# The odd mixer of a two-layer transformer block: keys and values in front of the last query slot, whose product and head chain stand beside the attention's first steps

## The reference, cut to what matters

```python
def odd_mixer(h_lat, h_ctx, w_in, w_out, qg, kg, cos, sin, need_ctx_out):
    q, k, v = split_cols(h_lat @ w_in, SIZES_ODD)          # 1024, 256, 256 columns
    q = apply_rope(rms_norm(q.reshape(B, S, H_C, HD_C), qg), cos, sin) * HD_C ** -0.5
    k = apply_rope(rms_norm(k.reshape(B, S, KV_C, HD_C), kg), cos, sin)
    v = v.reshape(B, S, KV_C, HD_C)
    ...
    ck, cv = split_cols(h_ctx @ w_in[:, H_C * HD_C:], SIZES_ODD[1:])
    ck = rms_norm(ck.reshape(B, L, KV_C, HD_C), kg)
    k_all = jnp.concatenate([ck, k], axis=1)
    v_all = jnp.concatenate([cv, v], axis=1)
    out_lat = block_attention(q, k_all, v_all) @ w_out     # softmax over 512 keys
```

## Time and profile before

| what | us |
|---|---|
| median of 3 runs (lowest, highest) | 1694.84 (1694.27, 1703.23) |
| the profiled execution's own time | 1694.8 |
| its span | 1693.2 |
| PE busy in it | 1547.2 (91%) |
| DVE busy | 577.5 (34%) |
| ACT busy | 341.5 (20%) |
| mean granted TensorE clock | 0.954 of full speed |

### The profile page before, as it was taken

One profiled execution on the slowest core, in us unless ns is written; L12 is line 12 of the kernel. 1 busy time (PEld: TensorE's weight loads), 2 busy tenths in 40 slices (PEclk: granted clock), 3 DMA queues, 4 the chain that ended last, 5 costly groups with the idle time before them and its releaser, 6 DMA issues.

```text
span 1693.2 us, 27222 instructions
## 1 busy us (share of the span) xinstructions
PE 1547.2 (91%) x11479; PEld 1107.5 (65%) x11479; DVE 577.5 (34%) x1412; ACT 341.5 (20%) x786; POOL 93.8 (6%) x144
## 2 busy tenths in 40 slices
PE   6999899999879999997896899999949898999997
PEld 5787678877734766655533799988836575655554
DVE  2614423333345238404515111111046643233333
ACT  1313211122141112115304000000142223010110
POOL 0010000000110000001100200000010000000000
PEclk9899999999989989997997999999979997999999
DMA  8365444556873431034520799999876032999996
GB/s 263 96 209 182 143 132 129 165 186 195 219 226 106 154 116 51 32 119 127 199 75 30 285 389 399 396 399 401 341 245 237 25 125 96 371 391 387 387 387 255
DMA packets 188232, 366.93 MB, mean 217 GB/s; under 512 B 19100, under 2 KB 145912, under 8 KB 172272
## 3 DMA queue, kind: packets, MB, share of 16 engines
q1 hardware_dynamic: 171552, 322.90, 53.6%
q0 software_dynamic: 10544, 32.48, 6.0%
q10 hardware_dynamic: 6048, 10.31, 1.7%
HBM read 345.26 MB, written 20.41 MB: 216 GB/s over the span
## 4 chain that ended last, share of the span: by engine, by line
PE 81%; DVE 8%; DMA 5%; ACT 3%; issue 2%; POOL 1%; SPq 0%; POOLq 0%; ACTq 0%; DVEq 0%
PE ps_proj L646 30%; PE ps_outp L646 10%; PE ps_proj L1210 8%; PE ps_outp L1210 8%; PE ps_score L1210 7%; PE ps_outp L1155 3%; DMA ring<-in_exp_w 3%; PE ps_turn L799 2%; PE ps_outp L1310 2%; PE ps_proj L772 2%; PE ps_score L817 1%; DVE both_probs L2142 1%; PE ps_score L646 1%; DMA ring<-in_w_in 1%; PE ps_score L869 1%
## 5 line engine op out<-in xcount | busy, mean ns | idle before, releaser
L646 PE MATMUL ps_proj<-h_t,ring 128*128 128x256 f32 (+1 forms) x1280 | 356.6, 438 | 8.0 <-DMA ring<-in_w_in 3.7
L646 PEld LDWEIGHTS ps_proj<-h_t,ring 128*128 128x128 f32 x1280 | 246.9, 195 | 112.0 <-issue 77.1
L1210 PE MATMUL ps_proj<-ring,arena 128*32 128x384 f32 (+2 forms) x1760 | 118.8, 386 | 6.3 <-ACT arena L1919 2.2
L1210 PEld LDWEIGHTS ps_proj<-ring,arena 128*32 128x32 f32 (+1 forms) x1760 | 103.9, 115 | 21.7 <-issue 12.6
L1210 PE MATMUL ps_score<-ring,arena 128*32 128x384 f32 (+2 forms) x1760 | 115.3, 381 | 1.3 <-DMA ring<-in_exp_w 1.3
L1210 PE MATMUL ps_outp<-ring,arena 128*32 128x384 f32 (+2 forms) x1504 | 112.7, 417 | 3.0 <-DVE arena L2523 2.1
L1210 PEld LDWEIGHTS ps_score<-ring,arena 128*32 128x32 f32 (+1 forms) x1760 | 98.4, 113 | 17.4 <-issue 8.9
L646 PE MATMUL ps_proj<-ring,h_t 128*128 128x256 f32 (+1 forms) x512 | 105.8, 364 | 0.4 <-ACT arena L1787 0.4
L1607 ACT ACTIVATE arena<-ps_proj 128x512 f32<-128x512 f32 (+1 forms) x68 | 39.0, 576 | 319.8 <-PE ps_proj L646 318.1
L646 PEld LDWEIGHTS ps_proj<-ring,h_t 128*128 128x128 f32 x512 | 92.1, 190 | 14.9 <-issue 3.5
L1210 PEld LDWEIGHTS ps_outp<-ring,arena 128*32 128x32 f32 (+1 forms) x1504 | 81.8, 114 | 26.5 <-DVE arena L2523 3.8
(11 more groups left out here) (354 smaller groups left out, 1844.9 us busy)
## 6 DMA issues: line engine op xcount, KB each, us to landing
ring<-in_exp_w SPq DMA_DIRECT2D x138, 1024.0 KB, 11.1
ring<-in_ada_w SPq DMA_DIRECT2D x48, 1024.0 KB, 5.6
ring<-in_w_in SPq DMA_DIRECT2D x30, 1024.0 KB, 6.3
arena<-in_exp_w SPq DMA_DIRECT2D x24, 1024.0 KB, 17.1
ring<-in_even_w_in SPq DMA_DIRECT2D x12, 1024.0 KB, 6.2
ring<-in_w_out SPq DMA_DIRECT2D x8, 1024.0 KB, 5.2
row_store<-in_exp_w SPq DMA_DIRECT2D x8, 1024.0 KB, 16.8
x_t<-in_exp_w SPq DMA_DIRECT2D x16, 512.0 KB, 16.4
```

Source lines behind the costliest of these rows:

```text
L646: last = pe.matmul(out, w, a, start=(i == 0), stop=(i == len(pairs) - 1))
L1210: last = pe.matmul(b[p0:p0 + pn, c0:c0 + wn], x_of(p0, lo, pn), w(w0, wn), start=first and p0 not in strip[:i], stop=done and p0 not in st ...
```

## The change

The six slots run in the order 0, 1, 2, 4, 5, 3 (`ODD_SLOTS`), and their weights are loaded in that order. The first five stand where they stood; the values and the fifth slot's `turn_pairs` follow; the sixth slot, the last pair of query heads (heads 6 and 7), moves into the attention. TensorE computes its product at the end of step 0 and its head sums and rotation at the end of step 2. ScalarE does its square and scaled copy behind the first softmax and its root behind the third. VectorE does its chain in step 3, between the copy of the transposes and the copy of the apply. The scores of head 0 wait for `head_ready` 13, those of head 6 for 14. The wait for the values' drain moves into the apply. `gv_slot` now marks the moved slot. No arithmetic is added or removed.

```diff
-        for c in range(6):
+        for c in (0, 1, 2, 4, 5, 3):
             add(((0, KC, 256), k_cols(dr["odd_w_in_2"][0], 256 * c, 256)))
...
+        ODD_SLOTS = (0, 1, 2, 4, 5, 3)
...
-            for c in range(6):
+            for s, c in enumerate(ODD_SLOTS[:5]):
...
-            mark["gv_slot"] = slot[0]
             token_major(h2, 4)
             k_gv = use["proj"]
-            turn_pairs(5)
-            got("proj", k_gv)
-            pe.wait_ge(head_ready, 14)
+            turn_pairs(4)
+
+            def last_queries():
+                mark["gv_slot"] = slot[0]
+                feature_major(h2, S, S)
+                mark["raw", 5] = use["proj"]
+
             units = []
             for h in range(8):
                 for t in range(NB):
                     def scores(h=h, t=t):
+                        if t == 0 and h in (0, 6):
+                            pe.wait_ge(head_ready, 13 if h == 0 else 14)
                         b = claim("score")
...
                     def apply(par, h=h):
+                        got("proj", k_gv)
                         b = claim("outp")
...
-            attention(units)
+            attention(units, {0: last_queries, 2: lambda: turn_pairs(5)})
...
+            def odd_slot(s):
+
+                b = take("proj")
+                if s >= 2:
+                    act.wait_ge(head_ready, 8 + s - 1)
+                head_square(b[:, :], g_sq)
+                row = ROW["gqa_q" if ODD_SLOTS[s] < 4 else "gqa_k"]
+                act.activation(raw[:, s % 2, :], b[:, :], ACT.Identity, scale=vec[:, row:row + 1]
+                               ).then_inc(drained["proj"], 1)
+
+            for s in range(5):
+                if s == 1:
                     rms_root(S)
                     stream_shift(1)
...
+                odd_slot(s)
+                if s >= 1:
+                    head_root(8 + s - 1, P, ODD_SLOTS[s - 1] >= 4)
             for t in (0, 2):
                 evac(gv[:, t:t + 2, :])
-            head_root(13, P)
+            head_root(12, P)
             warm_up(ACT.Exp)
-            for _ in range(16):
+            for i in range(16):
                 softmax([(0, T2)])
+                if i == 0:
+                    odd_slot(5)
+                if i == 2:
+                    head_root(13, P, False)
             warm_up(ACT.Sqrt)
...
-            for c in range(6):
-                dve.wait_ge(drained["proj"], mark["raw", c])
+            def turned_head(s):
+
+                c = ODD_SLOTS[s]
+                dve.wait_ge(drained["proj"], mark["raw", s])
                 b = take("outp")
...
+            for s in range(5):
+                turned_head(s)
...
-            attention(units)
+            attention(units, (range(3, 4), lambda part: turned_head(5)))
```

More of the change, by code:

```diff
@@ L1526, in _, with turn_pairs @@
             ready = mixer_input()
-            def turn_pairs(c):
+            def turn_pairs(s):
                 head_sums("ones", g_sq)
-                got("proj", mark["raw", c])
+                got("proj", mark["raw", s])
                 b = claim("outp")
-                chain(b[:, :], [(cst("rot2"), raw[:, c % 2, :])]).then_inc(filled["outp"], 1)
-            for c in range(6):
+                chain(b[:, :], [(cst("rot2"), raw[:, s % 2, :])]).then_inc(filled["outp"], 1)
+            for s, c in enumerate(ODD_SLOTS[:5]):
                 if c < 4:
@@ L1546, in _ @@
                         done_with("proj")
-                mark["raw", c] = use["proj"]
-                if c == 0:
+                mark["raw", s] = use["proj"]
+                if s == 0:
                     norm(h2[:, :, 0:S], S)(0, 4)
-                if c >= 1:
-                    turn_pairs(c - 1)
-            mark["gv_slot"] = slot[0]
+                else:
+                    turn_pairs(s - 1)
             token_major(h2, 4)
             k_gv = use["proj"]
-            turn_pairs(5)
-            got("proj", k_gv)
-            pe.wait_ge(head_ready, 14)
+            turn_pairs(4)
[3 more added lines that the diff above has]
+                mark["raw", 5] = use["proj"]
             units = []
@@ L2028, in _ @@
             stream_squares(1, mark["moe_done", 0])
-            for c in range(6):
-                if c == 1:
+            def odd_slot(s):
[8 more added lines that the diff above has]
+                if s == 1:
                     rms_root(S)
                     stream_shift(1)
[L2033 to L2041, removed]
+                odd_slot(s)
+                if s >= 1:
+                    head_root(8 + s - 1, P, ODD_SLOTS[s - 1] >= 4)
             for t in (0, 2):
                 evac(gv[:, t:t + 2, :])
-            head_root(13, P)
+            head_root(12, P)
             warm_up(ACT.Exp)
-            for _ in range(16):
+            for i in range(16):
                 softmax([(0, T2)])
+                if i == 0:
+                    odd_slot(5)
+                if i == 2:
+                    head_root(13, P, False)
             warm_up(ACT.Sqrt)
@@ L2786, in _ @@
             sin2 = cst("sin2").unsqueeze(1).to_broadcast([P, 2, S])
-            for c in range(6):
-                dve.wait_ge(drained["proj"], mark["raw", c])
+            def turned_head(s):
+                c = ODD_SLOTS[s]
+                dve.wait_ge(drained["proj"], mark["raw", s])
                 b = take("outp")
-                r = raw[:, c % 2, :]
-                rs = rsin[:, c % 2, :]
+                r = raw[:, s % 2, :]
+                rs = rsin[:, s % 2, :]
                 if c < 4:
@@ L2803, in _ @@
                     step(dve.tensor_tensor(r[:, lat], r[:, lat], rs[:, lat], ALU.add))
[L2804 removed]
+                head_rstd(8 + s)
                 dst = gq_t[:, 2 * c:2 * c + 2, :].rearrange("p a b -> p (a b)") if c < 4 else gk_t[:, c - 4, :]
                 dve.tensor_tensor(dst, r, rstd[:, :], ALU.mult).then_inc(head_ready, 1)
+            for s in range(5):
+                turned_head(s)
             units = []
```

## The result

The changed kernel took 1707.82 us (median of 20 runs, 1697.96 to 1714.16) against 1697.79 for the kernel before (20 runs, 1691.31 to 1706.91): ratio 1.0056, 95% interval 1.0043 to 1.0070. It is slower by 9.5 us, 7.3 to 11.9. The forecast was 1701.6, ratio 1.0040, and its range ended at 1707; the time lies above it. The profiled execution took 1701.29 us, with a span of 1699.7; of the 20 runs it is the second fastest.

What follows compares the result with a forecast made beforehand. TensorE carries 81% of the chain that ended last; the change acts only through its idle time. VectorE's stall +5.4 and the low clock +1.4 make +6.8 us on 1694.8: 1701.6 us, range 1694 to 1707.

Steps and rivals of the forecast that it cites:

- The hole: TensorE's idle time before the attention's first scores, filled by VectorE's key head chain: keeps 5.67 us, comes 8.62 us earlier.
- The moved product: Last query product, moved behind the attention's first scores: TensorE work costs the same on both sides, 6.90 us at full clock.
- The stall of step 3: Before transposes 3 TensorE idles 6.6 us (second idle time) for VectorE's 6.25 us head chain; +5.4 us up to there.
- The clock behind it: After TensorE's second idle time, before transposes 3: 3.45 us at 1.2 GHz make one step 3.9 us, +1.4 us.
- both clock terms: Low clock for 3.45 us after each restart: under the moved product until 1327.8, and behind the second idle time, +1.4 us.
- The rival of the low clock: Clock stays low through the attention's next steps, 1.4 us for each further step, giving 1704.4; chance 0.20.
- the base: Time of the kernel before: profiled execution 1694.8 us, taken as practically the median of the runs, 1694.84.
- within 0.5%: Whole kernel: chance 0.64 that the time changes by less than 0.5%, 8.5 us.
- -0.9 if the head chain cost nothing: Attention up to transposes 3: -0.9 us without VectorE's head chain cost, from the covered softmax of step 0.
- the ScalarE part: Moved slot's square, copy, root and table loads in the attention's first steps: covered, nothing; 3.3 us of cover at the root.
- Pass-through: From the attention's end to the kernel's end: a shift passes one to one, the stretch stays 315 us.

Runs made afterwards that it cites:

- early_turn: Kernel before with the last key head's sums, rotation and root moved in front of the values; 1691.34 us, ratio 0.9963.
- after_early: Changed kernel with the last key head's sums and rotation moved in front of the values; 1699.36 us, ratio 1.0006.
- chain_off: Changed kernel without the last query head pair's rotation and reciprocal on VectorE, four of five instructions; 1695.47 us, ratio 1.0002.
- double: Changed kernel with the last head's reciprocal done twice, 3.35 us more on VectorE in step 3; 1713.20 us, ratio 1.0071.
- late: Changed kernel with the last slot's head sums, rotation, root and VectorE chain at steps 8 and 9 instead of 2 and 3; 1705.99 us, ratio 1.0045.
- changed_again: The changed kernel measured once more without any edit; 1703.08 us, ratio 1.0048.
- order_only: Kernel before with the slots in the order 0, 1, 2, 4, 5, 3 and nothing moved into the attention; 1702.06 us, ratio 1.0015.

## Why the prediction was right or wrong

**The hole stays.** Right: 5.62 us for 5.67. It was VectorE's chain: early_turn, which only moves that chain's start, removes all but 0.69 us, the values' drain.

**The moved product costs the same on both sides.** Right at full clock: 6.90 forecast, 6.91 in after_early, and chain_off keeps the product and is level with before. In the changed kernel it takes 8.30, because it stands where the clock is low; the forecast had 7.76 there.

**The stall of step 3.** Right in place, cause and size. Forecast: transposes 3 at 1350.05 in the time of before; the stage started 0.69 us earlier after, so 1349.72 reads 1350.41 there, 0.36 late. Two small errors stand in that. TensorE was 0.68 late up to transposes 2, from the clock under the moved product, which came back 4.8 us behind the first scores and not 3.45. From transposes 2 to 3 it took 8.51 us and not the 8.83 that I had allowed. VectorE's five instructions took 6.25 us; double and late show that what stands in this chain is paid for in full, and in the middle of the attention too.

**The clock behind it. This is the step of the forecast that failed.** I carried the 3.45 us of low clock after the restart from the first idle time over to the second, for a term of 1.4 us, and put a longer one into a rival of 0.20. It was 6.0 us: the two steps took 4.32 and 3.27 for my 3.93 and 2.53, and the term is 2.54 us; 1.9 to 2.5 in the five profiles that have the stall without filling. The mistake was to count the low time from the restart. In before the clock had fallen 3.4 us before the first scores; in after it fell 0.9 us before transposes 3, so of the same 6.8 us of low clock more was left to be paid by the work. Nor is 6.8 us the same everywhere: it was 3.4 in the first low stretch of changed_again and 10.2 in order_only. So I could not have named the size from one row, only a wider bound. Why the clock falls late in one idle time and early in another no run here shows. With both clock terms the sum is 6.8 + 0.36 + 1.13 = 8.3, which is the 8.24 of the stretch. The rival of the low clock was thus half true: one further step, not two.

**The rest of the miss.** The time is 6.2 us over the forecast (1707.82 for 1701.6). Of that 3.0 is the base: I read 1694.84 as settled from three runs, of which one stood at 1703.23, and the median of 20 runs of the same kernel is 1697.79. 1.4 us are the two clock terms. The last 1.8 us, by which the two medians differ (10.0) more than the two stretches (8.24), no trace shows; the interval of 7.3 to 11.9 us holds the 8.24, and changed_again gives 1.0048 (8.1 us). The clock terms alone would have stayed inside the range; it needed all three to leave it, and it should have been wider on top by the scatter of the base. That the profiled execution took 1701.29 us, next to the forecast of 1701.6, is luck: it is 6.45 us over the profile of before, because it reached this stage 0.69 us earlier and took 1.05 us less behind it. The forecast of "within 0.5%" (0.64) was on the wrong side of the line by 0.06%; with the clock's term right it would have been 8.3 of 8.5 us, an even chance.

**"-0.9 if the head chain cost nothing".** Wrong. chain_off, with one fifth of the chain's instructions left, is 1.05 above before, not under it. Two things make up the difference of about 2 us. 1.3 is step 3: the reload of the exponential's table, which I had called covered, lies on the path as soon as VectorE's chain doesn't cover it. 0.7 is again the low clock under the moved product, longer than I had allowed. For the changed kernel itself the ScalarE part held: root at 1341.04, exponential at 1343.50, wanted at 1348.99. From its timeline of all engines:

```profile
1339.74 1.28 ACT L1614 ACT_TABLE_LOAD   x1 [1.05 <-PE ps_proj L647]
...
1341.04 0.60 ACT L1614 ACTIVATE root<-ps_proj 128x512 f32<-128x512 f32 x1
...
1343.50 0.69 ACT L1670 ACTIVATE both_probs<-ps_score,negmax 128x512 f32<-128x512 f32 x1
...
1348.99 0.15 DVE L2153 RECIPROCAL inv<-total 128x1 f32<-128x1 f32 x1
```

The rows show no drain beside the load here either (load at 1339.74, root 1.30 us later); the Trainium skill's 2.66 us for a switch (ScalarE: Activation LUTs, What ACT_TABLE_LOAD costs) is not borne out in these rows, and the measurement decides.

**Pass-through.** Right: 314.5 us from the attention's end to the span's end, 315 forecast, and 314 to 317 in nearly all kernels.

## What to carry to other kernels

Before moving work beside a loop, ask for every engine what room a step has, not only for the one that seems to bound the stage: here TensorE's product could be moved at no price at full clock, but VectorE had 0.25 us in a step of 2.53 and was given 6.25 at once. Look for what fills an idle time and move the start of that chain ahead of independent work: two moved lines in early_turn closed the hole that the larger change left open. Of work to cover a latency choose the kind that asks nothing of the engine on the chain, as the last quarter of the values did.

## What the runs showed of the hardware that I had not expected

A stretch of low clock may begin at the very end of an idle time and is then paid for almost wholly by the work behind it: in the changed kernel the clock was full for 5.3 us of TensorE's second idle time and low for 6.0 us of the work after it. How long it stays low varies too: behind idle times of 5.6 to 6.5 us it was back between 3.0 us (changed_again, first idle time) and 9.1 us (order_only) after the restart. Idle times of 5.6 to 6.2 us therefore cost between 0.9 and 2.9 us beyond themselves, and the cost differs by 0.9 us at the same idle time of one kernel (scores 0 to scores 1: 10.22 and 9.34). Filling such an idle time with products that nobody reads shortened the stretch by 2.4 us. And a float32 reciprocal of 128 x 512 on VectorE takes 3.35 us, nearly five times the 0.69 of a multiply of the same size; in quarters of 128 columns it is 0.94 each.
